# Order of the second block's projections: recurrent rows, gates, query-key-value, with ScalarE emptying the last two

## The chip, the cores and the metric

The kernel runs on one core of a Trainium2 chip. The metric is the device time of one execution, in microseconds (us). All numbers of the profile come from one execution taken by the hardware profiler; its engines are TensorE (PE; PEld for its weight loads), VectorE (DVE), ScalarE (ACT), GpSimd (POOL) and SyncE (SP), which issues nearly all DMAs.

## What is computed

Two different transformer blocks run one after the other on 256 tokens of 1024 channels, all in float32. The first block has two layers; the second has one. The change lies in the second block, whose start is this:

```
h = rms_norm(x, norm1_gain)
p = h @ w_in                                     # 1024 -> 6176 columns
q, k, v, p_rwkv, p_gate = split(p, [768, 768, 768, 1824, 2048])
q = rms_norm(heads(q), q_norm_gain);  k = rms_norm(heads(k), k_norm_gain)
# attention of 12 heads in 3 groups, with a bias from a table of distances -> y_att

prev = p_rwkv shifted by one token
pm = p_rwkv + (prev - p_rwkv) * shift_mu
r, k, v, xw, xa, xg = split(pm, [512, 512, 512, 64, 64, 160])
decay from tanh(xw) @ w_up;  a = sigmoid(a0 + xa @ a_up);  g = sigmoid(xg) @ g_up
kk = k * k_k, divided by its length per head;  k = k * (1 + (a - 1) * k_a)
o = recurrence over the tokens(r, decay, k, v, kk, a), head norm, + bonus(r, k, r_k, v), * g
y_rwkv = o @ w_rwkv_out

mixed = sigmoid(p_gate)[:, :1024] * y_att + sigmoid(p_gate)[:, 1024:] * y_rwkv
x = x + mixed @ w_out
x = x + mixture of 32 experts(rms_norm(x))       # every expert's weights are read
```

## The kernel before

All 256 tokens stay in on-chip memory as two tiles of 128 rows (T = 2). Each engine runs a program of its own, written out in order; they meet only through semaphores. An engine that waits holds back all that stands behind it in its own program.

The projection `h @ w_in` of the second block is cut into column blocks of at most 512: four recurrent ones ("rw", the last of 288 columns), five for query, key and value ("qkv", the last of 256) and four gate blocks. Each block's weights come in four pieces of 256 rows, 52 pieces in all. A float32 product is made from three products of rounded parts (lines 999 to 1001): for each piece ScalarE copies the high part out of the loaded weights (line 1707), GpSimd subtracts it to get the low part (`split_low`, line 869), and TensorE multiplies. There are six buffers for loaded pieces and four for split ones (`RAWS2`, `SPLITS2`): ScalarE may split piece j when TensorE has done piece j - 4, and SP may load piece j when GpSimd has done piece j - 6. The order of the pieces is that of `second_pieces`, and it sets the order of SP's loads, ScalarE's and GpSimd's splits and TensorE's products (`project`).

Results land in PSUM banks, which `second_plan` hands out: each unit (one block for one of the two row tiles) has its banks and the engine that empties it, "V" for VectorE or "A" for ScalarE. `begin` makes TensorE wait until the bank's last unit is emptied. Before the change recurrent and qkv units alternate between VectorE and ScalarE over four banks, and gate units are all ScalarE's.

TensorE's program in this part: the transposes of x, the rw blocks, one product for the bias by distance (line 1319), the qkv blocks, the transposes and products of the low-rank step (called lora, lines 1326 to 1338), the gate blocks, the transposes of q and k (line 1348), attention (lines 1359 to 1381), then the recurrent core. ScalarE's follows it: `while_projecting` runs the splits ahead of a block, its emptyings, and the splits behind; between qkv and gates come Sigmoid and Tanh of the lora inputs (lines 1904, 1905). After the first gate block it takes two square roots, one for the recurrent keys and one for the q and k norm (lines 1920, 1922).

VectorE's program: its rw emptyings (line 2378); the token shift in three passes over 3648 elements (lines 2387, 2389, 2391), the last of which signals `pm_ready`; its qkv emptyings (line 2394); the lora additions (line 2400) and squares of the recurrent keys (2409 to 2413); then the norm of q and k: squares and sums (2419, 2421), a wait for the square root, scaling (2427 to 2432), gains (2437), which signals `qk_ready`; then the recurrent preparation (2442 to 2458), which ends with `preproc_done`; then attention.

SP issues in one queue: the weight pieces in order, with other loads put in at named pieces: the three moves of the token shift at the seventh qkv piece, the seven row vectors (after `pm_ready`) at the fourteenth, and behind all pieces the load of the bias matrix, 1.5 MB:

```
sp.wait_ge(bias_stored, 16)
sp.wait_ge(qk_ready, 1)
sp.dma_start(bias_m, ...).then_inc(bias_loaded, 16)
units.wait_full(("gate", PROJ_GATE - 1))
```

It waits for `qk_ready` since `bias_m` lies over the memory of `qk_gain`. On TensorE the transposes of q and k wait for `bias_loaded` and `qk_ready`. Behind it SP issues the four loads of the output weights, and later those of the experts, each when a product has freed its buffer.

## Time and profile before

| | |
|---|---|
| median of 3 runs | 1596.62 us (1595.19 to 1598.37) |
| the profiled execution | 1589.97 us, its span 1588.1 us |
| instructions in the profile | 21720 |
| mean granted TensorE clock | 0.970 of full speed |
| busy share | TensorE 94%, VectorE 44%, ScalarE 34%, GpSimd 28% |
| DMA | 351.75 MB in 44399 packets, mean 221 GB/s |

The page of the profile lists busy time by engine, slices of the span, the DMA queues, the chain of work that ended last and the costliest groups of instructions. A row of the timeline is one instruction, or several of one kind in a run (xN): start, time, engine, line, operation, output and inputs with shapes, and in brackets the idle time of the engine ahead of it and what ended it. The span starts with the first instruction; times in rows count from there. Matmuls are pipelined, so the time from start to start tells more than the time of one. DMAs are issued by SPq; from issue to landing is told by a row of its own.

### The profile page before, as it was taken

What the parts mean: (1) busy time and instruction counts of PE and PEld (TensorE: products, weight loads), DVE (VectorE), ACT (ScalarE), POOL (GpSimd) and SP (SyncE); (2) the same over time, 40 slices, a digit from 0 to 9 for tenths busy, and PEclk for the clock granted to TensorE, in tenths of its full rate; (3) what the DMA queues carried; (4) which work ended last, traced back from release to release, by engine and by line L of the source; (5) the groups of instructions that cost most, each with busy time, mean ns of one, the idle gap of its engine ahead of it and who ended that gap; (6) DMA issues with size and microseconds to landing.
All of it is one profiled execution on the core that took longest, in us unless ns stands there. A gap on an engine that the chain in (4) does not pass through costs nothing.

```text
span 1588.1 us, 21720 instructions
## 1 busy us (share of the span) xinstructions
PE 1498.0 (94%) x8310; PEld 1089.1 (69%) x8310; DVE 694.4 (44%) x1081; ACT 544.0 (34%) x816; POOL 444.0 (28%) x160
## 2 busy tenths in 40 slices
PE   6989999998999999999889989998999999999998
PEld 6778899987778999987657669855453444443443
DVE  3785475555765655642418434733112112112112
ACT  5646533345556533334335421112111011011110
POOL 3372444343453343437968020100000000000000
PEclk9999999999999999999989979998999999999999
DMA  6341355554331456457663510006799999999994
GB/s 236 138 140 67 133 177 195 186 180 139 135 133 54 164 184 208 165 168 244 205 196 112 193 58 1 1 7 259 321 428 428 428 427 428 428 429 428 429 427 181
DMA packets 44399, 351.75 MB, mean 221 GB/s; under 512 B 5171, under 2 KB 7135, under 8 KB 19743
## 3 DMA queue, kind: packets, MB, share of 16 engines
q1 hardware_dynamic: 43630, 349.37, 57.5%
q8 instruction: 52, 0.85, 0.2%
q10 hardware_dynamic: 576, 1.13, 0.2%
q0 software_dynamic: 112, 0.17, 0.1%
q14 instruction: 29, 0.24, 0.0%
HBM read 347.71 MB, written 1.07 MB: 220 GB/s over the span
## 4 chain that ended last, share of the span: by engine, by line
PE 63%; DMA 17%; DVE 7%; issue 5%; ACT 2%; DVEq 2%; POOL 1%; SPq 0%; POOLq 0%; ACTq 0%
DMA ring<-in_w_expert_up 16%; PE psum L999 13%; PE psum L1000 13%; PE psum L1001 13%; PE psum L1612 9%; PE psum L988 3%; PE psum L1638 2%; PE psum L1578 1%; PE psum L1067 1%; PE psum L1451 1%; DVE arena L2117 1%; DVE arena L2160 1%; PE psum L1086 1%; DMA arena<-arena 1%; DVEq L2192 1%
## 5 line engine op out<-in xcount | busy, mean ns | idle before, releaser
L869 POOL TENSOR_TENSOR weights_split<-weights_raw,weights_split 128x2048 fp32r<-128x2048 f32 (+4 forms) x108 | 389.8, 3622 | 424.1 <-ACT weights_split L1707 423.9
L1707 ACT ACTIVATE weights_split<-weights_raw 128x2048 fp32r<-128x2048 f32 (+4 forms) x154 | 243.4, 1584 | 280.9 <-PE psum L1001 280.4
L1612 PE MATMUL psum<-ring,arena 128*64 128x512 f32 x1024 | 233.8, 612 | 17.4 <-DMA ring<-in_w_expert_up 16.3
L1612 PEld LDWEIGHTS psum<-ring,arena 128*64 128x64 f32 x1024 | 75.4, 140 | 172.6 <-issue 172.6
L999 PE MATMUL psum<-weights_split,h_split 128*128 128x512 f32 (+3 forms) x400 | 155.5, 389 | 15.8 <-DVE arena L2394 6.4
L1000 PE MATMUL psum<-weights_split,h_split 128*128 128x512 f32 (+3 forms) x400 | 153.7, 384 | 0.0
L1001 PE MATMUL psum<-weights_split,h_split 128*128 128x512 f32 (+3 forms) x400 | 153.3, 383 | 0.0
L999 PE MATMUL psum<-weights_split,hidden_split 128*128 128x512 f32 (+1 forms) x384 | 149.9, 390 | 1.5 <-DVE hidden_split L1695 1.5
L1000 PE MATMUL psum<-weights_split,hidden_split 128*128 128x512 f32 (+1 forms) x384 | 148.3, 386 | 0.0
L1001 PE MATMUL psum<-weights_split,hidden_split 128*128 128x512 f32 (+1 forms) x384 | 148.1, 386 | 0.0
L999 PE MATMUL psum<-h_split,weights_split 128*128 128x256 f32 x512 | 145.2, 284 | 1.4 <-DVE weights_split L869 1.4
L1000 PE MATMUL psum<-h_split,weights_split 128*128 128x256 f32 x512 | 144.9, 283 | 0.0
L1001 PE MATMUL psum<-h_split,weights_split 128*128 128x256 f32 x512 | 144.9, 283 | 0.0
L869 DVE TENSOR_TENSOR weights_split<-weights_raw,weights_split 128x2048 fp32r<-128x2048 f32 (+2 forms) x46 | 107.5, 2340 | 28.1 <-ACT weights_split L1707 27.4
L1638 PE MATMUL psum<-arena 128*64 128x512 f32 x512 | 113.4, 595 | 0.0
L999 PEld LDWEIGHTS psum<-weights_split,h_split 128*128 128x128 f32 x400 | 77.5, 194 | 34.7 <-issue 13.1
L999 PEld LDWEIGHTS psum<-h_split,weights_split 128*128 128x128 f32 x512 | 98.2, 192 | 2.5 <-DVE weights_split L869 1.8
L1000 PEld LDWEIGHTS psum<-h_split,weights_split 128*128 128x128 f32 x512 | 98.2, 192 | 0.5
L1001 PEld LDWEIGHTS psum<-h_split,weights_split 128*128 128x128 f32 x512 | 98.2, 192 | 0.0
L2748 DVE TENSOR_TENSOR arena<-psum,arena 128x512 f32<-128x512 f32 x16 | 11.1, 691 | 190.3 <-PE psum L1612 190.3
L2327 DVE TENSOR_TENSOR hidden_split<-arena,hidden_split 128x512 fp32r<-128x512 f32 x32 | 85.8, 2681 | 15.3 <-ACT hidden_split L1864 15.3
L1001 PEld LDWEIGHTS psum<-weights_split,h_split 128*128 128x128 f32 x400 | 77.6, 194 | 15.3
(370 smaller groups left out, 2113.5 us busy)
## 6 DMA issues: line engine op xcount, KB each, us to landing
weights_raw<-in_layer_w SPq DMA_DIRECT2D x94, 1024.0 KB, 4.8
ring<-in_w_expert_gate SPq DMA_DIRECT2D x32, 2048.0 KB, 16.2
arena<-in_w_expert_down SPq DMA_DIRECT2D x32, 2048.0 KB, 13.4
ring<-in_w_expert_up SPq DMA_DIRECT2D x32, 2048.0 KB, 17.1
weights_raw<-in_second_w SPq DMA_DIRECT2D x44, 512.0 KB, 4.5
weights_raw<-in_layer_w SPq DMA_DIRECT2D x6, 768.0 KB, 4.1
ring<-in_w_out SPq DMA_DIRECT2D x2, 2048.0 KB, 17.3
ring<-in_w_rwkv_out SPq DMA_DIRECT2D x1, 2048.0 KB, 9.9
```

Source lines behind the costliest of these rows:

```text
L869: eng.tensor_tensor(W.part(j, 1, n), W.raw(j, n), W.part(j, 0, n).bitcast(F32), ALU.subtract).then_inc(W.lo[W.pieces[j][1]], 1)
L988: ins = pe.matmul(bank[:, 0:n], lhs(i), w[:, i, :], start=(i == 0), stop=(i == k - 1))
L999: pe.matmul(out, a[0], b[0], start=first, stop=False)
L1000: pe.matmul(out, a[0], b[1], start=False, stop=False)
L1001: return pe.matmul(out, a[1], b[0], start=False, stop=last)
L1067: pe.matmul(bank[:, j * nk:(j + 1) * nk], qT_, kT_, start=True, stop=False)
L1086: ins = pe.matmul(bank[:, j * MLA_V:(j + 1) * MLA_V], probsT[g % 2][:, c * P:(c + 1) * P], v, start=(s == 0), stop=(s == t))
L1451: ins = pe.matmul(bank[:, c * P:(c + 1) * P], m[left_m][:, c, :], m[right_m][:, c, :], start=True, stop=True)
L1612: ins = pe.matmul(bank[half(j), :], xe[h][:, k, half(j)], w[j][:, k, :], start=(k == 0), stop=(k == KD - 1))
L1638: ins = pe.matmul(bank[half(j), :], hidT[:, f, half(j)], w[j][:, f, c * 512:(c + 1) * 512], start=(f == 0), stop=(f == D_EXP // P - 1))
L1707: act.activation(W.part(j, 0, w), W.raw(j, w), ACT.Copy).then_inc(W.hi, 1)
L2327: dve.tensor_tensor(part[1], hid_sq[i % 4], part[0].bitcast(F32), ALU.subtract).then_inc(hid_ready.sem, 1)
```

## The change

The order of the three projections becomes rw, gate, qkv. The plan of banks, the order of pieces and the programs of TensorE and ScalarE follow. Gate units take the banks (1, 2, 3, 0) that qkv units had and the other way round. All qkv units are now emptied by ScalarE, both row tiles, so VectorE's five instructions of line 2394 are gone and ScalarE has five more; the gates stay with ScalarE. The moves of the token shift keep their place by number among the pieces (the seventh after rw); the seven row vectors move from the fourteenth to the sixteenth after rw. On VectorE the recurrent preparation comes ahead of the q and k norm, which waits only for the units of the first three qkv blocks (all columns of q and k). On ScalarE the square root for the q and k norm comes after the last qkv emptying instead of after the first gate block.

```diff
--- before.py
+++ after.py
@@ -368,10 +368,10 @@
     plan = interleave("tr1", 4, (0, 1, 2, 3), "V")
     plan += interleave("rw", PROJ_RW, (4, 5, 6, 7), "VA")
     plan += interleave("bias", 1, (0,), "V")
-    plan += interleave("qkv", PROJ_QKV, (1, 2, 3, 0), "VA")
+    plan += interleave("gate", PROJ_GATE, (1, 2, 3, 0), "A")
     plan += interleave("loraT", T, (4, 5), "A")
     plan += interleave("lora", 3 * T, (6, 7, 4, 5, 6, 7), "VVA")
-    plan += interleave("gate", PROJ_GATE, (0, 1, 2, 3), "A")
+    plan += interleave("qkv", PROJ_QKV, (0, 1, 2, 3), "A")
     plan += interleave("qkT", 6, (4, 5, 6, 7), "A")
     for i in range(NA + 2):
         if i < NA:
@@ -412,7 +412,7 @@
 def second_pieces():
 
     return [((stage, b, i), "P", (stage, T * b + T - 1) if i == 3 else None)
-            for stage, cols in (("rw", RW_BLOCKS), ("qkv", QKV_BLOCKS), ("gate", GATE_BLOCKS))
+            for stage, cols in (("rw", RW_BLOCKS), ("gate", GATE_BLOCKS), ("qkv", QKV_BLOCKS))
             for b in range(len(cols)) for i in range(4)]
 
 
@@ -905,14 +905,14 @@
                     sp.dma_start(lora_w[LORA_W:P, 0, :], io["rwkv_a_up_2"][0]).then_inc(lora_loaded, 16)
                     sp.dma_start(lora_w[:, 1, :], io["rwkv_g_up_2"][0, 0:P, :]).then_inc(lora_loaded, 16)
                     sp.dma_start(lora_w[0:LORA_G - P, 2, :], io["rwkv_g_up_2"][0, P:LORA_G, :]).then_inc(lora_loaded, 16)
-                if name == ("qkv", 1, 2):
+                if name == ("gate", 1, 2):
                     units.wait_emptied(*(("rw", i) for i in range(PROJ_RW)))
                     sp.dma_start(prev[1:113, :, :], pf[0:112, :, :]).then_inc(prev_loaded, 16)
                     sp.dma_start(prev[113:P, :, :], pf[112:P - 1, :, :]).then_inc(prev_loaded, 16)
                     sp.dma_start(prev[0:1, 1, :], pf[P - 1:P, 0, :]).then_inc(prev_loaded, 16)
                     sp.wait_ge(bias_done, 1)
                     sp.dma_start(bias_dram, bias_row[0:ATT_H, :]).then_inc(bias_stored, 16)
-                if name == ("qkv", 3, 1):
+                if name == ("gate", 3, 3):
                     sp.wait_ge(pm_ready, 1)
                     for n in vec:
                         sp.dma_start(vec[n], row(n)).then_inc(vec_loaded, 16)
@@ -920,7 +920,7 @@
             sp.wait_ge(bias_stored, 16)
             sp.wait_ge(qk_ready, 1)
             sp.dma_start(bias_m, bass.AP(bias_dram.tensor, 0, [[1, P], [384, ATT_H], [1, SEQ]])).then_inc(bias_loaded, 16)
-            units.wait_full(("gate", PROJ_GATE - 1))
+            units.wait_full(("qkv", PROJ_QKV - 1))
             for name, _ in SW.blocks:
                 s = SW.where[name][0]
                 src, k, w = second_weight(name)
@@ -1318,7 +1318,7 @@
             bank, r = units.begin(("bias", 0)), slice(0, BUCKETS + ATT_H)
             units.finish(("bias", 0), pe.matmul(bank[0:ATT_H, 0:384], bias_tab[r, :], second("bucket_hot")[r, :],
                                                 start=True, stop=True))
-            project("qkv", QKV_BLOCKS)
+            project("gate", GATE_BLOCKS)
 
             pe.wait_ge(lora_in, 1)
             for t in range(T):
@@ -1336,7 +1336,7 @@
                 bank, rest = units.begin(("lora", 3 * t + 2)), slice(0, LORA_G - P)
                 pe.matmul(bank, loraT[:, 1, c], lora_w[:, 1, :], start=True, stop=False)
                 units.finish(("lora", 3 * t + 2), pe.matmul(bank, loraT[rest, 2, c], lora_w[rest, 2, :], start=False, stop=True))
-            project("gate", GATE_BLOCKS)
+            project("qkv", QKV_BLOCKS)
 
             pe.wait_ge(bias_loaded, 16)
             pe.wait_ge(qk_ready, 1)
@@ -1898,8 +1898,8 @@
             act.wait_ge(rstd2_ready, 1)
             for b, (c, w) in enumerate(RW_BLOCKS):
                 while_projecting("rw", b, lambda: empty(("rw", T * b + 1), pf[:, 1, c:c + w], w, scale=rstd_x[:, 1:2]))
-            for b, (c, w) in enumerate(QKV_BLOCKS):
-                while_projecting("qkv", b, lambda: empty(("qkv", T * b + 1), qkv[:, 1, c:c + w], w, scale=rstd_x[:, 1:2]))
+            for b, (c, w) in enumerate(GATE_BLOCKS):
+                while_projecting("gate", b, lambda: [empty(("gate", T * b + t), gates[:, t, c:c + w], w, ACT.Sigmoid, scale=rstd_x[:, t:t + 1]) for t in range(T)])
             act.wait_ge(pm_ready, 1)
             act.activation(pf[:, :, C_XG:RW_IN], pf[:, :, C_XG:RW_IN], ACT.Sigmoid)
             act.activation(pf[:, :, C_XW:C_XA], pf[:, :, C_XW:C_XA], ACT.Tanh).then_inc(lora_in, 1)
@@ -1913,13 +1913,13 @@
             act.wait_ge(wa_in, 1)
             act.activation(bufB, bufB, ACT.Sigmoid)
             act.activation(bufR, bufR, ACT.Sigmoid).then_inc(wa_ready, 1)
-            for b, (c, w) in enumerate(GATE_BLOCKS):
-                while_projecting("gate", b, lambda: [empty(("gate", T * b + t), gates[:, t, c:c + w], w, ACT.Sigmoid, scale=rstd_x[:, t:t + 1]) for t in range(T)])
+            for b, (c, w) in enumerate(QKV_BLOCKS):
+                while_projecting("qkv", b, lambda: [empty(("qkv", T * b + t), qkv[:, t, c:c + w], w, scale=rstd_x[:, t:t + 1]) for t in range(T)])
                 if b == 0:
                     act.wait_ge(kk_ss, 1)
                     act.activation(kk_n, kk_n, ACT.Sqrt).then_inc(kk_std, 1)
-                    act.wait_ge(qk_ss_ready, 1)
-                    act.activation(stat2[:, 0:48], stat2[:, 0:48], ACT.Sqrt, bias=eps_c, scale=1.0 / ATT_E).then_inc(qk_std, 1)
+            act.wait_ge(qk_ss_ready, 1)
+            act.activation(stat2[:, 0:48], stat2[:, 0:48], ACT.Sqrt, bias=eps_c, scale=1.0 / ATT_E).then_inc(qk_std, 1)
             for j in range(6):
                 dst = (qT, kT)[j // 3][:, 2 * (j % 3):2 * (j % 3) + 2, :].rearrange("p c s -> p (c s)")
                 empty(("qkT", j), dst, 512)
@@ -2389,10 +2389,6 @@
             dve.tensor_tensor(prev, prev, mu.unsqueeze(1).to_broadcast([P, T, RW_IN]), mul)
             dve.drain()
             dve.tensor_tensor(pf, pf, prev, add).then_inc(pm_ready, 1)
-            for b, (c, w) in enumerate(QKV_BLOCKS):
-                bank = units.wait_full(("qkv", T * b))
-                units.emptied_by(("qkv", T * b), dve.tensor_scalar(qkv[:, 0, c:c + w], bank[:, 0:w], rstd_x[:, 0:1], None, mul), "V")
-
             dve.wait_ge(vec_loaded, 16 * len(vec))
             for t in range(T):
                 for j, (dst, n) in enumerate(((bufR, "w0"), (bufB, "a0"))):
@@ -2412,7 +2408,29 @@
             dve.drain()
             dve.tensor_reduce(th(kk_n), heads(bufK), AX.X, add).then_inc(kk_ss, 1)
 
-            units.wait_emptied(*(("qkv", j) for j in range(PROJ_QKV)))
+            dve.wait_ge(kk_std, 1)
+            dve.wait_ge(wa_ready, 1)
+            dve.tensor_scalar(kk_n, kk_n, 1e-12, None, ALU.max)
+            dve.drain()
+            dve.reciprocal(kk_n, kk_n)
+            dve.drain()
+            dve.tensor_tensor(heads(bufA), heads(bufA), per_head(th(kk_n), hshape), mul)
+            for t in range(T):
+                dve.scalar_tensor_tensor(bufK[:, t, :], bufB[:, t, :], -1.0, vec["k_a"], add, mul)
+            dve.drain()
+            for t in range(T):
+                dve.scalar_tensor_tensor(k_[:, t, :], bufK[:, t, :], 1.0, k_[:, t, :], add, mul)
+            dve.tensor_tensor(bufB, bufB, bufA, mul)
+            dve.drain()
+            dve.tensor_tensor(bufK, r_, k_, mul)
+            dve.drain()
+            dve.tensor_tensor(bufK, bufK, channels("r_k"), mul)
+            dve.drain()
+            dve.tensor_reduce(th(bonus), heads(bufK), AX.X, add).then_inc(bonus_ready, 1)
+            dve.drain()
+            dve.sem_inc(preproc_done, 1)
+
+            units.wait_emptied(*(("qkv", j) for j in range(T * (2 * ATT_W // 512))))
             qk = [qkv[:, :, j * ATT_W:(j + 1) * ATT_W].rearrange("p t (h e) -> p t h e", e=ATT_E) for j in range(2)]
             sq = qk_sq.rearrange("p t (h e) -> p t h e", e=ATT_E)
             for j in range(2):
@@ -2436,28 +2454,6 @@
                     a = qk[j][:, t, :, :].rearrange("p (g h) e -> p g h e", g=GRP)
                     ins = dve.tensor_tensor(a, a, qk_gain[:, j, :, :].unsqueeze(2).to_broadcast([P, GRP, HPG, ATT_E]), mul)
             ins.then_inc(qk_ready, 1)
-
-            dve.wait_ge(kk_std, 1)
-            dve.wait_ge(wa_ready, 1)
...
-            dve.tensor_reduce(th(bonus), heads(bufK), AX.X, add).then_inc(bonus_ready, 1)
-            dve.drain()
-            dve.sem_inc(preproc_done, 1)
 
             for i in range(NA + 2):
                 if i < NA:
```

## Rows read from the trace of the kernel before

**Rows 1.** The profile page: busy time by engine, with shares of the span.

```profile
PE 1498.0 (94%) x8310; PEld 1089.1 (69%) x8310; DVE 694.4 (44%) x1081; ACT 544.0 (34%) x816; POOL 444.0 (28%) x160
```

**Rows 2.** Windows by stage; columns as in the first line.

```profile
core 0: us, PE busy (x) PEld busy (x) DVE busy (x) ACT busy (x) POOL busy (x), PEclk, DMA share, GB/s
759.00:818.20 59.20, 52.81 (x241) 43.15 (x240) 19.76 (x9) 21.69 (x24) 51.45 (x21) 0.94 0.67 221
818.20:834.50 16.30, 12.00 (x23) 3.41 (x23) 3.98 (x6) 4.92 (x10) 6.44 (x3) 0.69 0.45 129
834.50:879.40 44.90, 44.90 (x194) 36.04 (x193) 39.32 (x22) 22.50 (x26) 36.44 (x12) 1.00 0.36 106
...
1100.00:1588.00 488.00, 459.54 (x2355) 214.67 (x2354) 95.06 (x278) 67.38 (x122) 0.00 (x0) 0.98 0.92 389
```

**Rows 3.** TensorE's waits, 670 to 945: us in total, times, longest.

```profile
PE psum L999 <- DVE arena L2394: 6.4, 1, 6.4
...
PE psum L999 <- POOL weights_split L869: 3.4, 1, 3.4
```

**Rows 4.** Timeline of TensorE at the third qkv block.

```profile
788.07 0.77 PE L999 MATMUL psum<-weights_split,h_split 128*128 128x512 f32 x1 [6.39 <-DVE arena L2394]
...
792.89 0.39 PE L999 MATMUL psum<-weights_split,h_split 128*128 128x512 f32 x1
```

**Rows 5.** Timeline of VectorE, token shift: first and last of three.

```profile
770.84 4.31 DVE L2387 TENSOR_TENSOR arena<-arena 128x3648 f32<-128x3648 f32 x1 [11.17 <-DMA arena<-arena]
...
781.31 5.95 DVE L2391 TENSOR_TENSOR arena<-arena 128x3648 f32<-128x3648 f32 x1
```

**Rows 6.** Timelines of GpSimd, one of each window; x2 is two pieces.

```profile
772.67 10.78 POOL L869 TENSOR_TENSOR weights_split<-weights_raw,weights_split 128x1024 fp32r<-128x1024 f32 x2 [1.33 <-ACT weights_split L1707]
...
777.38 12.10 POOL L869 TENSOR_TENSOR weights_split<-weights_raw,weights_split 128x1024 fp32r<-128x1024 f32 x2
...
783.41 8.39 POOL L869 TENSOR_TENSOR weights_split<-weights_raw,weights_split 128x1024 fp32r<-128x1024 f32 x2
...
797.09 2.41 POOL L869 TENSOR_TENSOR weights_split<-weights_raw,weights_split 128x1024 fp32r<-128x1024 f32 x1 [0.38 <-ACT weights_split L1707]
```

**Rows 7.** Windows around stretches of the granted clock; columns as in rows 2.

```profile
734.30:737.80 3.50, 3.50 (x11) 2.72 (x10) 0.00 (x0) 0.00 (x0) 3.50 (x2) 0.51 0.59 161
785.50:792.40 6.90, 4.33 (x10) 3.51 (x11) 3.08 (x3) 0.00 (x0) 6.90 (x3) 0.51 0.39 115
823.10:833.30 10.20, 9.82 (x14) 2.54 (x14) 2.85 (x5) 0.84 (x3) 1.54 (x1) 0.50 0.36 104
879.40:915.20 35.80, 32.93 (x187) 22.61 (x186) 13.73 (x34) 16.86 (x39) 0.00 (x0) 1.00 0.55 205
```

**Rows 8.** Timeline of ScalarE between the last qkv product and lora.

```profile
818.35 0.47 ACT L1875 ACTIVATE arena<-psum,stat 128x256 f32<-128x256 f32 x1 [0.29 <-PE psum L1001]
...
819.78 1.28 ACT L1904 ACT_TABLE_LOAD   x1
```

**Rows 9.** Timeline of TensorE: the first transpose of lora.

```profile
821.80 0.33 PE L1326 MATMUL psum<-shared_c,arena 128*128 128x128 f32 x1 [3.49 <-ACT arena L1905]
```

**Rows 10.** Timeline of SP: the issue of the bias load.

```profile
868.30 0.39 SPq L922 DMA_DIRECT2D arena<-bias_by_distance  x1
```

**Rows 11.** DMA issues: KB each, median us from issue to landing.

```profile
arena<-bias_by_distance SPq DMA_DIRECT2D x1, 1536.0 KB, 6.7
```

**Rows 12.** Timeline of TensorE: the transposes of q and k.

```profile
879.40 2.78 PE L1348 MATMUL psum<-shared_c,arena 128*128 128x128 f32 x24
```

**Rows 13.** Timeline of VectorE: operations of the norm, and one in the core.

```profile
836.76 1.75 DVE L2419 TENSOR_TENSOR arena<-arena 128x1536 f32<-128x1536 f32 x1
...
850.27 5.63 DVE L2432 TENSOR_TENSOR arena<-arena,stat 128x1536 f32<-128x1536 f32 x2
855.98 12.24 DVE L2437 TENSOR_TENSOR arena<-arena 128x768 f32<-128x768 f32 x4
...
1022.30 0.69 DVE L2516 TENSOR_TENSOR arena<-arena,stat 128x512 f32<-128x512 f32 x1
```

More of the change, by code:

```diff
@@ L2438, in _ @@
             ins.then_inc(qk_ready, 1)
-            dve.wait_ge(kk_std, 1)
-            dve.wait_ge(wa_ready, 1)
-            dve.tensor_scalar(kk_n, kk_n, 1e-12, None, ALU.max)
-            dve.drain()
-            dve.reciprocal(kk_n, kk_n)
-            dve.drain()
-            dve.tensor_tensor(heads(bufA), heads(bufA), per_head(th(kk_n), hshape), mul)
-            for t in range(T):
-                dve.scalar_tensor_tensor(bufK[:, t, :], bufB[:, t, :], -1.0, vec["k_a"], add, mul)
-            dve.drain()
-            for t in range(T):
-                dve.scalar_tensor_tensor(k_[:, t, :], bufK[:, t, :], 1.0, k_[:, t, :], add, mul)
-            dve.tensor_tensor(bufB, bufB, bufA, mul)
-            dve.drain()
-            dve.tensor_tensor(bufK, r_, k_, mul)
-            dve.drain()
-            dve.tensor_tensor(bufK, bufK, channels("r_k"), mul)
-            dve.drain()
-            dve.tensor_reduce(th(bonus), heads(bufK), AX.X, add).then_inc(bonus_ready, 1)
-            dve.drain()
-            dve.sem_inc(preproc_done, 1)
             for i in range(NA + 2):
```

## Prediction

> **What bounds the kernel now.** I first read the page's totals: TensorE is busy 94% of the span [rows 1], so what counts is where TensorE stands idle or slow, and after that what it waits for. The windows by stage [rows 2] cut the second block at the change: recurrent rows and query-key-value up to 818.2, the low-rank step (lora) 818.2 to 834.5, gates up to 879.4, then attention and the recurrent core. The last row, 1100 to the end, has the DMA engines 0.92 busy: that tail streams the experts, but its loads are released by products of the stages ahead, so a microsecond lost before 1100 comes out at the end as a microsecond. The gates stage has TensorE busy for all of its 44.9 us, 16 pieces of weights: 2.8 us for a piece of 512 columns. Only two waits in the stages concerned are long [rows 3]: 6.4 us for VectorE (line 2394, the emptying of query-key-value) and 3.5 us for ScalarE (line 1905, the Tanh ahead of the lora transposes) [rows 9].
>
> **The first wait, and what comes in its place.** TensorE stops after 781.3 and resumes at 788.07, the third query-key-value block, whose bank VectorE has not emptied [rows 4]. VectorE is in the three long operations of the token shift from 770.84 to 787.3 [rows 5]. With gates in this place, emptied by ScalarE alone, that wait goes. But GpSimd, which makes the low halves of the weights (line 869), is late too: undisturbed such a piece takes 2.41 us, while here its starts are 772.67, 777.38, 783.41 and (6.0 later) 789.44 [rows 6], since GpSimd and VectorE take turns; one piece is 2.4, and the rest is the VectorE operation it stood behind. Counting the pieces from the first recurrent one (0), these are 23, 24 and 25. Piece 24 is thus split at 783.4 and piece 25 at 789.5, and the change moves neither: the token shift, its loads and the places in SP's queue are the same pieces as before. So TensorE starts piece 24 at 783.5 instead of 788.07, waits 3 us, starts 25 at 789.5, and then runs on at 2.8 with GpSimd back at 2.4. Before, piece 25 began at 792.9, because piece 24 ran at half clock (4.8 us) after the idle time [rows 4, 7]. Gain 3.4 us. The clock may fall again through the new gaps (2.0 and 3.1 us); the gap of 3.4 us for GpSimd in the recurrent rows was followed by 3.5 us at 0.51 [rows 3, 7], which costs about 1.6. Within piece 24 that is free, since 25 isn't split. I take 0.8: gain 2.6, bounds 1.0 and 3.4.
>
> The Trainium skill (SBUF — State Buffer, Who interferes with whom) says that a VectorE instruction with two SBUF inputs and a GpSimd instruction that reads SBUF lock each other out for a whole instruction, and that a reduction never contends. The trace agrees: the three pieces above are lengthened by the long operations beside them. What hangs on it is the length of the norm's operations once no splits run: by this rule they shrink as worked out below; if they keep their length, the time is that of the second rival, 1623.
>
> **The lora wait.** Before the transposes ScalarE does, after the last product: an emptying at 818.35, a weight split, a table load at 819.78 (1.28), Sigmoid, Tanh; TensorE resumes at 821.8, 3.6 us after the end of the projections [rows 8, 9]. After the change Sigmoid has been in use for the gates, so the load leaves this place (it moves to the first gate block, where ScalarE waits for TensorE in any case), and the emptying is of 512 columns, 0.2 longer. The wait becomes 2.5: gain 1.1. For the load the trace has 1.28, and the next activation starts right behind it. The lora step itself is unchanged: TensorE was at clock 0.50 for 10.2 us of it [rows 7]. If a shorter wait kept it at full clock, 5.1 us would go; the row nearest is this very one and it speaks for the same fall, so I take 0, bound 5.1.
>
> So the projections end earlier. Gate end: 789.5 + 7 x 2.8 + 0.8 = 809.9; transposes at 812.4; 12.7 for transposes and lora (821.8 to 834.5) [rows 2, 9]: query-key-value starts at 825.1. It takes 50.6: the 59.2 of its stage before, less 6.6 of wait and 2.0 of slow clock [rows 2, 4]. It ends at 875.7, against 879.4: **3.7 earlier**.
>
> **What moves on to the path.** Before, the query and key norm (lines 2419 to 2437) ran under the gates; its last operation ended at 868.2 [rows 13], the bias load was issued at 868.30 and took 6.7 us to landing [rows 10, 11], and the transposes of q and k (line 1348) followed the gates at 879.40 without a gap [rows 12]. They wait for the bias load, and that load waits in SP's queue for the end of the norm, because it overwrites the gains. In the new order the norm can't end before the last q and k are emptied, and its square root on ScalarE comes after the last emptying of all. The gates, 44.9 us of cover, are gone from behind it; only the value columns (16.8 us) are left.
>
> Worked through: ScalarE's square root for the recurrent keys comes after the first block: 825.1 + 11.2, an emptying, a split and the table load, 839.9. Then VectorE does the recurrent preparation. It has eight operations of two SBUF inputs (lines 2446 to 2456) of about 1.1 (1024 elements) or 0.6 us (512), from 1.75 for 1536 elements undisturbed [rows 13], 7.0 in sum. Behind continuous splits each waits for a piece: 8 x 2.36 more. With 2.6 for the small ones and the reduction: ends at 868.4. Squares and sums for the norm, four of 1.7 with two waits of 1.1: 877.2. This is 0.7 later than ScalarE's last emptying, so VectorE's chain is the late one, narrowly. Square root 0.4: 877.6. Then the rest of the norm, with no splits left: small ones 0.7, two multiplications of 1536 elements at 1.6 (traced at 2.8 beside the splits), four of 768 at 0.8 (traced at 3.1 each, 12.24 in all, which is one split of 2.36 and 0.7): 7.1 us, 884.7 [rows 6, 13]. That a broadcast from a small operand costs nothing extra is read from line 2516: 0.69 for 512 elements [rows 13]. Bias load: 0.1 + 6.7. Transposes at **891.5 instead of 879.4: 12.1 later**, after some 16 us in which TensorE does nothing. The four loads that SP issues behind the bias load (output weights, 7 MB by their shapes) wait for the last projection; before they came 11 us after it, now they follow at once, behind it in the same queue; I charge 0 (bounds 0 and 3).
>
> What is queued behind: on TensorE all of attention and the recurrent core; on SP the output weights (needed only behind attention, so covered); on ScalarE the transposes' emptyings; on VectorE the row maxima. GpSimd has nothing until then.
>
> Two supplies in the qkv stage are narrow: hand-stepping the splits as above leaves each piece 0.6 us or more before TensorE wants it (the same stepping of the gates stage gives 0.5, and there TensorE had no gap [rows 2]), so I charge nothing, bound 3.
>
> **The clock after the gap.** After the 6.6 us gap TensorE ran at half until 792.4, 4.3 us past its resumption [rows 4, 7]. The transposes take 2.78 us at full clock [rows 12] and about 5 at half; the first scores follow at half too. Before, attention began at full clock [rows 7]. Cost 3, bounds 0 and 7.
>
> **Sum.** -3.7 (end of projections) + 15.8 (gap from there to the transposes) + 3.0 (clock) = +15.1, on a span of 1588.1, whose execution took 1589.97; 6.65 less than the median of 1596.62. I put the difference on the median: 1596.6 + 15.1 = **1611.7**. A measurement here can tell 0.2%, 3.2 us, from no change.
>
> **Rivals.** (1) As above, the bias load and norm bare: 1611.7, chance 0.75. (2) The norm's operations keep their traced durations (their slow access being their own and not GpSimd's): 5.63 + 12.24 against 6.4, 11.5 more: 1623. For it: all four of line 2437 are alike; against: the splits beside them are too, at 3.1. Chance 0.06. (3) GpSimd becomes the bound in the last projection: eight preparation operations against pieces wanted every 2.8 us cost TensorE 3, and the norm, which VectorE reaches later, another 2: 1617. The margin of 0.6 is for it; against it, the gates stage stood the same load before [rows 2]. Chance 0.13. (4) Not slower: the gapless projections. If GpSimd were ready for pieces 24 and 25, TensorE wouldn't stop at all at 781.5, and the clock would hold through gates and lora: 8.6 there, 1.1 for the table load, 5.1 in lora, 14.8 in all, against 15.8 and no clock loss after: +1, 1598. It decides from where a split takes under 2.8 us during the token shift; the rows have 6.0. Chance 0.06, of which 0.02 falls below -0.2%.
>
> **Range.** Low: lora at full clock and half of the clock charge gone, 1611.7 - 5.1 - 2.3 = 1604.3. High: rival 3 with the bias load 3 late, 1620. Faster 0.02, same 0.04, slower 0.94.
>
> **What would show it.** Right: no wait for line 2394; two short waits of TensorE on GpSimd (line 869) in the second gate pieces; no table load ahead of the Tanh; TensorE idle some 16 us ahead of line 1348, with SP waiting for line 2437 and the bias load landing last; line 2437 at under 1 us each; half clock at the transposes. Wrong: q and k transposes that start right behind the last projection, or a gap under 10 us.

## The result and the profile after

The changed kernel takes 1612.8 us (median of 7 runs, 1604.7 to 1615.7) against 1594.0 us for the kernel before (median of 7). The ratio over all runs is 1.0104, 95% interval 1.0082 to 1.0126: slower by 16.6 us of 1594 (13 to 20), where the two medians alone are 18.8 us apart. The forecast was 15.1 us slower. The profiled execution took 1604.84 us, its span is 1603.0, 14.9 over that of before.

TensorE's longest waits in the changed kernel, 670 to 960 us (us in total, times, longest), answer to [rows 3, 9]:

```profile
PE psum L1348 <- DMA arena<-bias_by_distance: 16.6, 1, 16.6
PE psum L999 <- POOL weights_split L869: 8.2, 3, 3.4
PE psum L1400 <- DVEq L2485: 2.9, 1, 2.9
PE psum L1326 <- ACT arena L1905: 2.3, 1, 2.3
```

The wait for VectorE's emptying is gone, GpSimd's splits hold TensorE twice instead (8.2 us less the old wait of 3.4), the lora wait is 1.2 shorter, and ahead of the transposes of q and k there are 16.6 us where there was nothing. TensorE's timeline has the two waits for GpSimd at pieces 24 and 25:

```profile
788.10 0.50 PE L999 MATMUL psum<-weights_split,h_split 128*128 128x512 f32 x1 [1.82 <-POOL weights_split L869]
...
794.12 0.79 PE L999 MATMUL psum<-weights_split,h_split 128*128 128x512 f32 x1 [2.97 <-POOL weights_split L869]
```

The chain behind the 16.6 us is in three timelines of the changed kernel: VectorE's, ScalarE's, then SP's.

```profile
877.99 1.75 DVE L2439 TENSOR_REDUCE stat<-arena 128x24 f32<-128x1536 f32 x1
880.21 0.45 DVE L2445 RECIPROCAL stat<-stat 128x48 f32<-128x48 f32 x1 [0.47 <-ACT stat L1922]
...
880.99 3.43 DVE L2450 TENSOR_TENSOR arena<-arena,stat 128x1536 f32<-128x1536 f32 x2
884.49 3.56 DVE L2455 TENSOR_TENSOR arena<-arena 128x768 f32<-128x768 f32 x4
```

```profile
879.32 0.47 ACT L1875 ACTIVATE arena<-psum,stat 128x256 f32<-128x256 f32 x1 [0.22 <-PE psum L1001]
879.77 0.33 ACT L1922 ACTIVATE stat<-stat 128x48 f32<-128x48 f32 x1
```

```profile
888.13 0.39 SPq L922 DMA_DIRECT2D arena<-bias_by_distance  x1
```

The last product is issued at 879.01; the last emptying and VectorE's sums end within 0.1 us of each other at 879.8; the rest of the norm takes until 888.05; the load is issued at once and lands 7.7 us later. TensorE's timeline, to be held against [rows 12], and three windows (columns as in [rows 2]: span, busy times by engine, granted clock, DMA share, GB/s):

```profile
895.92 4.39 PE L1348 MATMUL psum<-shared_c,arena 128*128 128x128 f32 x24 [16.64 <-DMA arena<-bias_by_distance]
```

```profile
793.30:800.10 6.80, 5.98 (x14) 4.72 (x15) 0.00 (x0) 0.40 (x1) 6.80 (x4) 0.50 0.56 159
820.60:824.00 3.40, 3.32 (x6) 1.03 (x6) 1.17 (x2) 0.00 (x0) 0.21 (x1) 0.51 0.52 157
882.10:899.20 17.10, 3.28 (x16) 3.28 (x17) 5.88 (x6) 1.61 (x3) 0.00 (x0) 0.50 0.58 200
```

The span's start does not serve to compare the two: the first recurrent piece starts at 717.45 instead of 712.85, in a part whose instructions are the same (other stretches of half clock in the first block). So 4.6 of the 14.9 us are not the change's in this execution. From that piece on, in us, by the start of TensorE's instructions (E0 is a second profile of the changed kernel, E5 to E7 are experiments below):

| | before | changed | E0 | E5 | E6 | E7 |
|---|---|---|---|---|---|---|
| last product of the projections | 166.3 | 161.6 | 161.4 | 162.6 | 152.0 | 161.7 |
| transposes of q and k | 166.5 | 178.5 | 178.4 | 162.8 | 168.3 | 178.1 |
| first scores | 170.4 | 183.7 | 183.6 | 166.7 | 173.4 | 181.9 |
| cumulative products (line 1389) | 207.4 | 218.8 | 220.4 | 201.8 | 208.5 | 217.0 |
| recurrent core (line 1424) | 232.6 | 241.9 | 243.4 | 225.5 | 232.2 | 239.5 |
| first gather of the experts | 391.9 | 401.0 | 408.9 | 384.6 | 391.3 | 398.6 |
| last instruction | 875.2 | 885.5 | 891.9 | 868.0 | 875.3 | 884.8 |

### The profile page after: what moved, and what is told of

It reads as the page before. It is cut to its first block, busy times and chain, and to the rows that moved or that the text cites. A ratio compares the mean times of both kernels' runs of the same rounds, so it can differ in the third digit from the quotient of the medians.

```text
span 1603.0 us, 21718 instructions
## 1 busy us (share of the span) xinstructions
PE 1494.3 (93%) x8310; PEld 1091.3 (68%) x8310; DVE 695.4 (43%) x1076; ACT 546.6 (34%) x820; POOL 442.7 (28%) x160
## 4 chain that ended last, share of the span: by engine, by line
PE 61%; DMA 18%; DVE 8%; issue 5%; DVEq 3%; ACT 2%; POOL 2%; SPq 0%; POOLq 0%; ACTq 0%
DMA ring<-in_w_expert_up 17%; PE psum L999 13%; PE psum L1000 12%; PE psum L1001 12%; PE psum L1612 9%; PE psum L988 3%; PE psum L1638 1%; POOL weights_split L869 1%; PE psum L1578 1%; PE psum L1067 1%; PE psum L1451 1%; DVE arena L2117 1%; DVE arena L2160 1%; DVE stat L2170 1%; PE psum L1086 1%
## 5 line engine op out<-in xcount | busy, mean ns | idle before, releaser
L1612 PE MATMUL psum<-ring,arena 128*64 128x512 f32 x1024 | 234.1, 612 | 17.9 <-DMA ring<-in_w_expert_up 16.7
L999 PE MATMUL psum<-weights_split,hidden_split 128*128 128x512 f32 (+1 forms) x384 | 151.7, 395 | 0.0
L1000 PE MATMUL psum<-weights_split,hidden_split 128*128 128x512 f32 (+1 forms) x384 | 150.2, 391 | 0.0
L1001 PE MATMUL psum<-weights_split,hidden_split 128*128 128x512 f32 (+1 forms) x384 | 150.0, 391 | 0.0
## 6 DMA issues: line engine op xcount, KB each, us to landing
ring<-in_w_expert_gate SPq DMA_DIRECT2D x32, 2048.0 KB, 16.2
arena<-in_w_expert_down SPq DMA_DIRECT2D x32, 2048.0 KB, 13.7
```

The costliest lines, as they stand in the source:

```text
L999: pe.matmul(out, a[0], b[0], start=first, stop=False)
L1000: pe.matmul(out, a[0], b[1], start=False, stop=False)
L1001: return pe.matmul(out, a[1], b[0], start=False, stop=last)
L1612: ins = pe.matmul(bank[half(j), :], xe[h][:, k, half(j)], w[j][:, k, :], start=(k == 0), stop=(k == KD - 1))
```

## Experiments

Theory: the norm's end, ScalarE's square root and the bias load have lost their cover and stand in series ahead of attention. Rivals: GpSimd's splits are the bound; the norm's operations are slow in themselves; the clock makes the difference.

**E0, the changed kernel once more.**

> The changed kernel once more, unaltered, for a second profile of it beside the next three on one chip. Its profiled execution had a span 14.9 us over that of before, of which 4.6 us lie ahead of the second block's projections (the first recurrent piece starts at 717.45 and not 712.85), so 10.3 us belong to the change there; the medians are 17 us apart. If the start of the second block only wanders from execution to execution, a second profile can show another split. Expected: wait ahead of line 1348 of 16.5 us again, first part of the span anywhere within 5 us, time 1604 to 1616.

Ratio 1.0078 (1.0049 to 1.0108). By the ratio that is 12.4 us over the kernel before (8 to 17), 4 us less than in the first measurement, and the intervals overlap: the forecast of 15.1 lies between the two. E0 ran on the same chip and beside the same runs of the kernel before as E3, E4 and E7, so each of these is compared with it as well below; "under the changed kernel" by itself means against the ratio of 1.0104. The wait is there again (16.7 us), the table above agrees to 0.2 us up to the first scores, and then E0 loses 7.9 us by the first gather, with a stretch of 13.7 us at half clock on the way. TensorE's windows (us, busy, granted clock, DMA share, GB/s) in E0, then in the first profile of the same program:

```profile
1001.00:1015.00 14.00, 14.00 (x68) 0.51 0.01 1
955.00:1100.00 145.00, 140.53 (x908) 0.95 0.09 34
```

```profile
1001.00:1015.00 14.00, 14.00 (x129) 1.00 0.00 1
955.00:1100.00 145.00, 140.52 (x935) 1.00 0.15 57
```

Half as many products start in the same 14 us, with TensorE busy in both. From the core's start to the first gather it is 165.5 us in E0 and 159.1 in the first profile. So executions of one program differ by 6.4 us in the recurrent core alone, with the clock as the difference that the traces show; single spans say little here, and I lean on waits and on intervals.

**E1, the bias load freed from the norm.**

```
-        qk_gain = area(24600, ...)
+        qk_gain = area(22104, ...)
             sp.wait_ge(bias_stored, 16)
-            sp.wait_ge(qk_ready, 1)
```

> The changed kernel with the gains of the q and k norm moved to memory that the bias matrix does not cover, so that the bias load no longer waits for the end of the norm. Exposed-chain theory: the load lands under the value columns, and only the norm is left in TensorE's gap ahead of line 1348: 16.6 - 7.8 (SP's issue and 7.7 us of load) = 8.8 to 9.3 us. Time 7 to 9 us (0.5%) under the changed kernel, so about 0.5% over the kernel before. Rival (the gap is the clock's or GpSimd's, or another load ends late): the gap stays above 14 us and the time within 3 us of the changed kernel.

Ratio 1.0064 (1.0045 to 1.0082): 6.4 us under the changed kernel, slightly less than expected. The wait is now for the norm and as long as forecast:

```profile
PE psum L1347 <- DVE arena L2454: 8.9, 1, 8.9
```

The load is worth 7.7 of the 16.6 us. (Lines are one lower here.)

**E2, the norm ahead of the preparation on VectorE.** The block of lines 2413 to 2429 of the changed kernel moved behind `qk_ready`.

> The changed kernel with VectorE's old order: the q and k norm ahead of the recurrent preparation. If VectorE's late chain (squares that end behind the last emptying, as predicted by 0.7 us) sets the gap, it shrinks by 0.7 us; if ScalarE's last emptying and the square root behind it set it, it stays at 16.6 within 0.5. Either way the time is that of the changed kernel within 3 us. If the preparation, standing in the way of GpSimd's splits, cost TensorE anything, the projection of q, k and v gets shorter than 50.6 us; I expect the same 50.6, and four gains (line 2455 of the changed kernel) that still take 0.9 us each. The preparation itself, now without splits beside it, takes about 9 us in place of 27.

By the trace as expected: wait 16.5 us, end of the projections 161.6 and first gather 401.0 after the first piece, the same as without the edit. VectorE's timeline shows the sums ending at 871 and then waiting 9.41 us for ScalarE:

```profile
869.22 1.75 DVE L2417 TENSOR_REDUCE stat<-arena 128x24 f32<-128x1536 f32 x1
880.38 0.45 DVE L2423 RECIPROCAL stat<-stat 128x48 f32<-128x48 f32 x1 [9.41 <-ACT stat L1922]
...
884.67 3.56 DVE L2433 TENSOR_TENSOR arena<-arena 128x768 f32<-128x768 f32 x4
888.15 0.17 DVE L2438 TENSOR_SCALAR stat<-stat 128x16 f32<-128x16 f32 x1
...
896.33 1.22 DVE L2454 TENSOR_REDUCE stat<-arena 128x16 f32<-128x1024 f32 x1
```

So in the changed kernel the two chains are level, and taking VectorE's away gives nothing. The preparation takes 9.4 us here, without splits beside it, and 27.1 in the changed kernel (843.32 to 870.42), of whose VectorE timeline these are the first and last rows:

```profile
843.32 0.94 DVE L2413 TENSOR_SCALAR stat<-stat 128x16 f32<-128x16 f32 x1 [11.46 <-ACT stat L1920]
...
869.20 1.22 DVE L2429 TENSOR_REDUCE stat<-arena 128x16 f32<-128x1024 f32 x1
```

Its times missed: ratio 1.0143 (1.0113 to 1.0173) on four runs, 6 us over the changed kernel where I had allowed 3, though the intervals of the two overlap. The profiled execution shows nothing that would cost this; the other three had mean clocks of 0.959 to 0.962 against its 0.969. Which instructions lost the clock in them no profile shows.

**E3, square root early as well.** On ScalarE the wait for `qk_ss_ready` and the square root stand ahead of the fourth block's emptyings, on top of E2.

> The changed kernel with the norm ahead of the recurrent preparation on VectorE and, on ScalarE, the norm's square root ahead of the fourth block's emptyings instead of behind the last one. Exposed-chain theory: the norm's rest (7.6 us, 8 to 11 where splits still run beside it) now lies under the value columns, and what is left in the gap is SP's issue and the 7.7 us of bias load: the wait ahead of line 1348 falls from 16.5 to 8 to 10 us, and the time by 7 to 9 us (0.5%). Rival (the load is not the last thing, or it is slowed under the projection's weight loads): over 12 us.

The wait is as forecast. The ratio is 1.0058 (1.0031 to 1.0085), 7.3 us under the changed kernel but only 3.2 under E0 beside it, with intervals that overlap: the shorter wait is shown, a gain of 7 us in time is not.

```profile
PE psum L1348 <- DMA arena<-bias_by_distance: 9.5, 1, 9.5
```

**E4, E3 and E1 together.**

> The last one with the gains moved as well, so that neither the norm's rest nor the bias load stands behind the last emptying. Exposed-chain theory: the two parts add up: the wait ahead of line 1348 falls from 16.5 to under 2 us, the clock stays at full speed there, and the second block keeps what the change gains ahead of it (5.7 us to the end of the projections, by the two profiles). Time 15 to 19 us under the changed kernel, so 0 to 3 us under the kernel before (ratio 0.998 to 1.000). Rival (the norm was hidden better before, and something else, such as the row maxima or splits locked out by VectorE, comes late now): a wait of 5 us or more in the same place.

The wait in this place is 1.8 us, but the time misses: 1.0064 (1.0020 to 1.0108), 10 us over the upper end of what I expected. Five runs lie between 1593.0 and 1598.9 us (mean clocks 0.969 to 0.973), four between 1611.0 and 1621.4 (0.951 to 0.962). A wait of 3.7 us that I had not foreseen is visible. TensorE's waits:

```profile
PE psum L1370 <- ACTq L1935: 3.7, 1, 3.7
...
PE psum L1347 <- DVE arena L2434: 1.8, 1, 1.8
```

The preparation now stands between the norm and the row maxima on VectorE and holds the first softmax (line 1370 turns its exponentials); the expectation's rival had named row maxima, and the DMA wait had hidden it in E2. The profiled execution, which has this wait, took 1593.0 us, no more than the kernel before; the rest of the miss comes from the four long runs. They have the lower mean clocks, but no profile of one shows where.

**E5, one part alone, in the old order.** ScalarE empties both row tiles of every qkv block.

```
-    plan += interleave("qkv", PROJ_QKV, (1, 2, 3, 0), "VA")
+    plan += interleave("qkv", PROJ_QKV, (1, 2, 3, 0), "A")
-                while_projecting("qkv", b, lambda: empty(("qkv", T * b + 1), ...))
+                while_projecting("qkv", b, lambda: [empty(("qkv", T * b + t), ...) for t in range(T)])
-            for b, (c, w) in enumerate(QKV_BLOCKS):
-                bank = units.wait_full(("qkv", T * b))
-                units.emptied_by(("qkv", T * b), dve.tensor_scalar(...), "V")
```

> The kernel before, old order, with one part of the change alone: ScalarE empties both row tiles of every query-key-value block. GpSimd theory: the wait of 6.4 us for VectorE goes, and two waits on line 869 of about 2.2 and 3.4 us come in its place; piece 25 starts 3.4 us earlier. With a clock loss of up to 3 us behind it, the time is 0.4 to 3.4 us under the kernel before (ratio 0.998 to 1.000). Rival (nothing holds TensorE but the bank): no wait there, 8.5 us earlier, ratio 0.994 to 0.995.

Ratio 0.9978 (0.9965 to 0.9992), 3.5 us under the kernel before: this part of the change is a small gain by itself. The waits for GpSimd are the changed kernel's, to 0.1 us, and the lora wait is the old 3.5, since the table load stays where it was:

```profile
PE psum L999 <- POOL weights_split L869: 8.2, 3, 3.4
PE psum L1326 <- ACT arena L1905: 3.5, 1, 3.5
```

Nothing like the rival's 8.5 us appears: GpSimd takes over from the bank.

**E6, the token shift left out.** The three passes of VectorE are gone (a bare `sem_inc(pm_ready, 1)` in their place).

> The changed kernel without the three passes of VectorE over 3648 elements that mix each token with the one before (the token shift is left out, so the recurrent branch is computed from unshifted values). Their loads stay. Lock theory: GpSimd's pieces 23 to 25 take 2.4 us each like the others, TensorE has no wait in the gates, and the 5.6 us of waits and about 2.9 us of slow clock behind them go: 8 us (0.5%) under the changed kernel. If loss of clock in the low-rank step hangs on these waits too, up to 3 us more. Rival (GpSimd late for another reason, such as the loads of weight pieces): the waits on line 869 stay and the time is within 3 us of the changed kernel.

Ratio 1.0032 (1.0005 to 1.0059), 11.5 us under the changed kernel. Only the old wait for GpSimd is left, that in the recurrent rows, and the clock holds through gates and lora (windows, columns as above):

```profile
PE psum L999 <- POOL weights_split L869: 3.4, 1, 3.4
```

```profile
764.00:811.00 47.00, 46.52 (x200) 36.55 (x199) 1.06 (x2) 23.81 (x27) 42.12 (x18) 1.00 0.83 277
812.00:821.00 9.00, 7.39 (x23) 2.58 (x24) 3.33 (x5) 2.38 (x9) 2.35 (x1) 1.00 0.42 117
```

The gates end 8.0 us earlier and the projections 9.6. It is VectorE's passes that make GpSimd late, and with the gaps gone the half clock is gone too. The Trainium skill (SBUF — State Buffer, Who interferes with whom) has a lock of this kind, between a VectorE instruction with two inputs in SBUF and a GpSimd instruction that reads SBUF. E2 and E6 agree: the same operations take 9.4 us without GpSimd beside them and 27.1 with it, and without VectorE's passes no split is late. The wait ahead of the transposes of q and k is still 16.1 us here, so it does not hang on the token shift.

**E7, idle products in the gap.** 34 products into the bank that the transposes take next.

```
+            bridge(pe, units, ("qkT", 0), 34)
             pe.wait_ge(bias_loaded, 16)
```

> The changed kernel with 34 idle products of 256 columns (ident times a constant, in the bank that the transposes of q and k take next, overwritten by them) put in TensorE's gap ahead of line 1348; nothing else. They keep TensorE busy for some 15 us without doing anything, so the wait for the bias load is as long by the clock on the wall and only the granted clock can change. Clock theory: no stretch of half clock there (17.1 us of it before), the transposes take 2.8 us instead of 4.6 or so, and the row maxima start 1.3 to 3 us earlier after the load: time 1 to 5 us under the changed kernel. Rival (the clock costs nothing here): within 1 us of the changed kernel. If the products last longer than the gap, they add what they overhang, which the profile would show.

Ratio 1.0057 (1.0038 to 1.0076), 7.5 us under the changed kernel, more than the 5 allowed, but 3.3 under E0 beside it, which is within them. TensorE's timeline (each product stands as two instructions; the first row shows the last 50 of 68, which begin at 874.8):

```profile
878.70 10.96 PE L962 MATMUL psum<-shared_c 128*128 128x256 f32 x50
891.12 2.84 PE L1349 MATMUL psum<-shared_c,arena 128*128 128x128 f32 x24 [1.46 <-DMA arena<-bias_by_distance]
```

The transposes take 2.84 us again instead of 4.39. From the transposes to the first scores it is 3.8 us against 5.2, and the second block reaches the gather 2.4 us earlier than in the first profile of the changed kernel, 10.3 earlier than in E0. All seven runs lie between 1599.6 and 1604.4, where the changed kernel's eleven, E0's among them, lie between 1604.0 and 1615.7. That the filled gap is what keeps the executions together is not shown: E4, E8 and E9 have next to no gap in this place, and their runs spread over 17 to 28 us, E5's over 8.

**E8, everything early.** The changed order on VectorE, with E1, the early square root of E3, and the keys' square root ahead of the first qkv block.

> The changed kernel, VectorE in the changed order (preparation ahead of the norm), with three things moved off the end of the projections: the gains' memory (bias load free), the norm's square root ahead of the fourth block's emptyings, and the square root of the recurrent keys ahead of the first block instead of behind it, so that the preparation starts 10 us earlier and ends before q and k are there. Exposed-chain theory: the wait ahead of line 1348 is under 2 us and the 3.7 us of the kernel with the norm first, whose preparation stood ahead of the row maxima, are gone too; from the first recurrent piece to the first gather of the experts it takes 3 to 5 us less than the kernel before (391.9) where the clock is alike: time 0.2 to 0.4% under it. Rival (the preparation lasts 27 us beside the splits and holds the norm or GpSimd): a wait of 3 us or more.

A miss: the wait is 3.5 us, and the ratio 1.0020 (0.9994 to 1.0046), no difference to the kernel before that can be told. VectorE's timeline:

```profile
864.77 3.65 DVE L2437 TENSOR_TENSOR arena<-arena 128x1536 f32<-128x1536 f32 x1 [6.05 <-ACT arena L1874]
...
876.08 4.53 DVE L2450 TENSOR_TENSOR arena<-arena,stat 128x1536 f32<-128x1536 f32 x2
880.68 3.56 DVE L2455 TENSOR_TENSOR arena<-arena 128x768 f32<-128x768 f32 x4
```

The preparation is over at 858.7, 6 us before q and k, so it holds nothing; but the norm, from the third block's emptying at 864.7 to 884.2, is 19.5 us long, and the value columns' last product ends at 880.86, 16.2 us behind its start. I had counted the cover and not the chain that has to fit under it. The 3.7 us of E4 are gone, as expected.

**E9, E5 with ten idle products in the lora wait.**

> The kernel before in its old order, with ScalarE emptying all query-key-value units (ratio 0.9978 in an earlier run), and ten idle products in TensorE's 3.5 us of wait ahead of the lora transposes, in the bank that these take next. Clock theory: the 3.4 us stretch at half clock in the lora step goes, 1.5 to 2 us less than that kernel: ratio 0.996 to 0.997. Rival (the fall there comes from the lora products themselves): the same 0.998.

Locally as the clock theory has it: clock 1.00 through the lora step, whose products (TensorE's timeline; compare 2.07 each in the kernel before) take 1.1:

```profile
829.81 1.13 PE L1336 MATMUL psum<-arena 64*128 64x512 f32 x4 [0.81 <-ACT arena L1910]
830.87 1.13 PE L1338 MATMUL psum<-arena 128*128 128x512 f32 x2
```

But the ratio is 0.9990 (0.9965 to 1.0015), not 0.996 to 0.997, and the profiled execution, the longest of the twelve, had 34.1 us of half clock in the recurrent core (window 950 to 1100 at 0.89). In that execution the 2.4 us that it was ahead of E5 at the core's start were lost several times over in the core; of the others no profile tells. **The best version measured is E5**, the only one whose interval lies wholly under the kernel before; E9's overlaps it.

## Why the prediction was right

By its steps, on the two profiles, counted from the first recurrent piece.

| step | predicted | measured |
|---|---|---|
| piece 25 starts | 3.4 earlier | 3.4 earlier (794.12 - 717.45 against 792.89 - 712.85) |
| clock behind it, gates | +0.8 | +2.8 (6.8 us at 0.50) |
| lora wait | -1.1 | -1.2 |
| lora step | 0 (bound -5.1) | -3.1 (9.6 us, 12.7 before) |
| end of the projections | -3.7 | -4.8 |
| length of the qkv stage | 50.6 | 50.5 |
| from there to the transposes, more than before | 15.8 | 16.7 (16.9 less 0.2) |
| transposes later by | 12.1 | 11.9 |
| clock behind the gap | +3 (0 to 7) | -1.6 in one profile, +4.8 in E0 |

**The first wait** came out as stepped: TensorE pauses for 2.0 and 3.1 us on the splits of pieces 24 and 25 (2.2 and 3.4 from start to start, less the 0.23 of a product), the very numbers of the prediction, since GpSimd's places don't move. **Its clock term** was too small by 2.0: the half clock came not in piece 24, where it would have been free, but from 793.3 on, under pieces that had nothing to wait for. **The lora step** erred the other way. I took the row nearest, 10.2 us at half; the changed kernel has 3.4, E6 with no gaps none. The bound was right, the value not, and the two errors cancel to 1.0.

**The new gap** was sized by parts: ScalarE's and VectorE's chains level (0.7 apart predicted, under 0.1 measured), 0.7 us behind the last product where 1.5 were predicted, rest of the norm 7.1 predicted and 7.8 measured, bias load 6.7 and 7.7. The norm's shrinking is what ruled out the second rival: four gains in 3.56 us, where [rows 13] have 12.24. E1 and E3 each take their part away and the wait falls by 7.7 and 7.1; together (E4) to 1.8. That settles the cause of the wait. What made the load 1.0 us longer stays open. I had put 0 for the four loads behind it, with a bound of 3; but with them 0.4 us behind, the load took 7.7 (changed kernel), 7.6 (E3) and 7.2 (E6, E7), and with the next one 11 us or more behind 6.7 (before, E5), 7.1 to 7.4 (E1, E4, E8) and 8.5 (E9).

**The third rival** (GpSimd the bound in the last projection) didn't happen: TensorE is busy for all of the 50.5 us. **The fourth** has its first half right: E6 shows that without VectorE's passes there is no gap, and the clock holds in lora. It fails on its condition: the splits do take 6 us during the token shift.

**The clock behind the gap** is the term that the trace of before could only bound. Up to the first scores it costs 1.3 us (transposes 4.39 instead of 2.78). Behind that it depends on the execution. From the first scores to the core's start the first profile wins 3.9 us against the kernel before (which ran 17 us at half there) and E0 2.4; from there to the first gather the first profile is level, and E0 loses 6.2. From the transposes (+11.9 in both) to the end (+10.3, +16.7) this is -1.6 and +4.8. So the mechanism of the prediction held, but its last digit is partly luck: the sum of 15.1 hit 16.6 (13 to 20) and E0's 12.4 (8 to 17) with this term in the middle of its bounds, not because it was known, and with two clock terms ahead of it whose errors cancel.

What the clock does in the core stays open. The gap ahead of the transposes does not sort it: of the kernels with a wait of 16 us there, the first profile, E2 and E6 hold full clock from 955 to 1090 us and E0 has 13.7 us at half; E1 and E3 (8.9 and 9.5 us) have 13.7 as well; of those with next to none, E4, E5 and E7 hold it and E8 and E9 have 34.1.

## What to carry to other kernels

When a stage is moved to the end of a phase, list what comes only after its last result and in series (an emptying, a root, a norm, a load that waits for the norm's memory), size it without the contention that it had under cover, and compare it with the cover that is left; a wait that only guards memory, like the bias load's, is the cheapest link to take out. When a bank's wait is removed, look at the next producer in the same stretch: here the splits were late behind the same VectorE operations, and of 6.4 us 3.4 were won. And where executions of one program differ by their clock, judge an edit by its waits in the trace and by many runs, not by one span, and measure the kernel that it is compared with beside it: two measurements of the changed kernel were 4 us apart here.

## What the runs showed of the hardware

- A recurrent core of small products, TensorE busy 97% of it by the profile, ran at full clock in seven of the twelve profiles, but with 13.7 us at half in those of E0, E1 and E3 and 34.1 us in those of E8 and E9. E0 and the first profile of the changed kernel have the same instructions. Runs of E8 spread from 1589.5 us (mean clock 0.972) to 1610.5 (0.960).
- In the changed kernel TensorE's idle times of 1.8 and 3.0 us were followed by 6.8 us at half clock, and the 2.3 us ahead of the lora transposes by 3.4. In E6, where the first two gaps are gone, the same 2.3 us were followed by none.
- VectorE's preparation takes 9.4 us alone and 27.1 beside GpSimd's splits: each of its eight operations with two inputs in on-chip memory is 1.9 to 2.2 us longer there (a split is 2.4), while the splits beside it last 2.7 to 3.4 us.
- The load of 1.5 MB in pieces of 1 KB took 6.7 to 8.5 us from issue to landing. The loads issued behind it do not explain the difference: it was longest in E9, where the next one came 11 us later.
